# Modulation units of a two-block transformer kernel: 27 of them on VectorE, none in the norms' pauses, turned later and in other PSUM banks

## The reference

```python
c_act = jax.nn.silu(c)
for i in range(DEPTH):                                          # 2 layers
    mod = (c_act @ mod_w[i] + mod_b[i]).reshape(B, 3, 3, D)     # 9216 values a layer
    shift, scale, gate = mod[:, :, 0], mod[:, :, 1], mod[:, :, 2]
    h = modulate(rms_norm(x, norm_g[i, 0]), shift[:, 0], scale[:, 0])
    x = x + 0.5 * gate[:, 0, None, :] * swiglu(h, ffn_w_gate[i, 0], ffn_w_up[i, 0], ffn_w_down[i, 0])
    h = modulate(rms_norm(x, norm_g[i, 1]), shift[:, 1], scale[:, 1])
    y = fox_attention(h, ...) if i == 0 else dilated_attention(h, ...)
    x = x + gate[:, 1, None, :] * y
    h = modulate(rms_norm(x, norm_g[i, 2]), shift[:, 2], scale[:, 2])
    x = x + 0.5 * gate[:, 2, None, :] * swiglu(h, ffn_w_gate[i, 1], ffn_w_up[i, 1], ffn_w_down[i, 1])
```

## Time and profile before

| | |
|---|---|
| time, median of 3 runs | 2241.78 us (2241.42 to 2245.81) |
| profiled execution | 2246.45 us, of which the span of its instructions is 2244.8 us |
| busy: TensorE, its weight loads, VectorE, ScalarE, GpSimd | 96%, 84%, 66%, 48%, 7% |
| mean granted clock of TensorE | 0.987 of full speed |
| chain of work that ended last | TensorE 87%, ScalarE 5%, VectorE 5% |

### The profile page before, as it was taken

One profiled execution on the slowest core, in us unless ns is written; L12 is line 12 of the kernel. 1 busy time (PEld: TensorE's weight loads), 2 busy tenths in 40 slices (PEclk: granted clock), 3 DMA queues, 4 the chain that ended last, 5 costly groups with the idle time before them and its releaser, 6 DMA issues.

```text
span 2244.8 us, 33167 instructions
## 1 busy us (share of the span) xinstructions
PE 2149.6 (96%) x14132; PEld 1892.1 (84%) x14132; DVE 1484.3 (66%) x1939; ACT 1084.6 (48%) x1220; POOL 147.5 (7%) x180
## 2 busy tenths in 40 slices
PE   7999898999999999899999999999999999999998
PEld 5998665998799778687799887897998878988996
DVE  4677666776677666666665455567786655677874
ACT  4443465443444344645544335644555357435552
POOL 0311110111011100000000011000000110000000
PEclk9999999999999999999999999999999999999999
DMA  9977662977687756245275565534655564436551
GB/s 346 300 274 252 251 230 76 299 262 262 202 279 271 245 206 215 86 156 182 87 230 179 197 224 169 169 123 165 208 182 196 177 222 132 169 136 220 178 180 55
DMA packets 264259, 448.62 MB, mean 200 GB/s; under 512 B 11520, under 2 KB 147008, under 8 KB 263856
## 3 DMA queue, kind: packets, MB, share of 16 engines
q1 hardware_dynamic: 246784, 382.93, 51.5%
q0 software_dynamic: 17040, 62.46, 7.7%
q10 hardware_dynamic: 288, 1.11, 0.1%
HBM read 445.40 MB, written 1.06 MB: 199 GB/s over the span
## 4 chain that ended last, share of the span: by engine, by line
PE 87%; ACT 5%; DVE 5%; issue 1%; DMA 1%; POOL 0%; SPq 0%; ACTq 0%; DVEq 0%; POOLq 0%
PE ps L1494 85%; DVE wlo L1924 2%; ACT whi L1719 2%; PE ps L1685 1%; PE ps L1652 1%; ACT S L1719 1%; ACT L1719 1%; ACT xs L1719 1%; ACT xhi L1719 0%; DMA raw<-in_fox_w_in 0%; DMA raw<-in_mod_w 0%; PE ps L1642 0%; DVE S L2072 0%; DVE x L1974 0%; PE ps L1602 0%
## 5 line engine op out<-in xcount | busy, mean ns | idle before, releaser
L1924 DVE TENSOR_TENSOR wlo<-raw,whi 128x2048 fp32r<-128x2048 f32 (+1 forms) x339 | 769.6, 2278 | 402.8 <-ACT whi L1719 402.6
L1719 ACT ACTIVATE whi<-raw 128x2048 fp32r<-128x2048 f32 (+1 forms) x339 | 640.9, 1895 | 389.8 <-PE ps L1494 361.3
L1494 PE MATMUL ps<-xhi,whi 128*128 128x256 f32 x2632 | 650.5, 287 | 8.1 <-DVE wlo L1924 3.5
L1494 PE MATMUL ps<-xhi,wlo 128*128 128x256 f32 x2632 | 644.7, 285 | 0.0
L1494 PEld LDWEIGHTS ps<-xhi,whi 128*128 128x128 f32 x2632 | 508.8, 193 | 14.2 <-issue 4.8
L1494 PEld LDWEIGHTS ps<-xhi,wlo 128*128 128x128 f32 x2632 | 509.1, 193 | 1.8 <-issue 1.4
L1494 PE MATMUL ps<-xlo,whi 128*128 128x256 f32 x2632 | 344.3, 283 | 0.1
L1494 PEld LDWEIGHTS ps<-xlo,whi 128*128 128x128 f32 x2632 | 327.6, 192 | 0.5 <-DVE xlo L2038 0.3
L1494 PE MATMUL ps<-whi,xhi 128*128 128x512 f32 x736 | 297.1, 404 | 18.2 <-ACT xhi L1719 11.2
L1494 PE MATMUL ps<-wlo,xhi 128*128 128x512 f32 x736 | 291.3, 396 | 0.0
L1494 PE MATMUL ps<-whi,hhi 128*128 128x512 f32 x528 | 211.3, 400 | 5.7 <-DVE hlo L2048 4.1
(11 more groups left out here) (233 smaller groups left out, 1942.0 us busy)
## 6 DMA issues: line engine op xcount, KB each, us to landing
raw<-in_w_in SPq DMA_DIRECT2D x52, 1024.0 KB, 5.1
raw<-in_ffn_w_gate SPq DMA_DIRECT2D x88, 512.0 KB, 4.7
raw<-in_ffn_w_up SPq DMA_DIRECT2D x88, 512.0 KB, 5.9
raw<-in_ffn_w_down SPq DMA_DIRECT2D x44, 1024.0 KB, 5.0
raw<-in_w_up SPq DMA_DIRECT2D x88, 512.0 KB, 4.9
raw<-in_dil_w_in SPq DMA_DIRECT2D x36, 1024.0 KB, 5.2
raw<-in_mod_w SPq DMA_DIRECT2D x28, 1024.0 KB, 7.0
nbuf<-in_mod_w POOLq DMA_DIRECT2D x44, 512.0 KB, 5.2
```

What stands on the lines that cost most here:

```text
L1494: return nc.tensor.matmul(o, lhs, rhs, start=start, stop=stop, skip_group_check=True)
L1719: return nc.scalar.activation(o, i, func, **kw)
L1924: V.tensor_tensor(wlo[:, s["c"], 0:s["n"]], raw[:, s["slot"], 0:s["n"]], whi[:, s["c"], 0:s["n"]].bitcast(F32), ALU.subtract).then_inc(sem ...
```

## The change

- The first FFN gets 9 units on VectorE, the second and the third 8, the fourth 2: 27. Five fewer are computed on TensorE.
- No unit is computed in a norm's pause (`in_norm` goes, with its two pieces in the weight stream).
- The forgetting attention's projections have three units, one after each, instead of four; the dilated attention's have two instead of one.
- In FFN (0,0) `run_work` takes two and three parts in turn in the up projection (`work_rate`), elsewhere two as before.
- There is a third sum `macc`, in the last quarter of `xs`.
- The first down piece (`down(0)`) no longer lowers the counts of finished units (`age=False`), so a unit that ended with the up projection is turned behind that piece, in G3 or G2, and not ahead of it.
- After a norm whose turned x lay in G0, G1, D0, D1 the second projection's banks are (G0, G1), before (G2, G3).

```diff
@@ __init__
-        self.acc_free = [None, None]
+        self.acc_free = [None] * 3
+        self.work_turn, self.work_rate = 0, (2, 2)
@@ run_turns, run_work
-    def run_turns(self, mod_only=False):
+    def run_turns(self, mod_only=False, age=True):
...
-        for entry in self.acc_turns:
+        for entry in self.acc_turns if age else ():
             entry[0] -= 1
...
-    def run_work(self, n=2):
+    def run_work(self, n=None):
+        n, self.work_turn = n or self.work_rate[self.work_turn], 1 - self.work_turn
@@ mod_part
-        acc = self.n_units % 2
+        acc = self.n_units % 3
@@ begin_units
-        self.pair = 0
-        self.first_pair = (D2, D3) if self.turn_banks[0] == G0 else None
+        self.pair = int(self.turn_banks[0] == G0)
+        self.first_pair = (D2, D3) if self.pair else None
@@ down
         if q == 0:
-            self.run_turns()
+            self.run_turns(age=False)
@@ Tail
-        plan.run_work(len(plan.work))
+        plan.run_work(len(plan.work) + 1)
@@ stage_order
-        in_norm = {("ffn", 0, 1): (0, 16), ("ffn", 1, 0): (1, 6), ("ffn", 1, 1): (1, 16), ("mix", 0): (0, 11), ("mix", 1): (1, 14)}
-        on_vector = {(0, 0): [(0, u) for u in range(4, 11)], (0, 1): [(0, 17)] + [(1, u) for u in range(6)],
-                     (1, 0): [(1, u) for u in range(7, 14)], (1, 1): [(1, 17)]}
-        fill = {0: [(0, u) for u in range(12, 16)], 1: [(1, 15)]}
+        on_vector = {(0, 0): [(0, u) for u in range(4, 13)], (0, 1): [(0, 16), (0, 17)] + [(1, u) for u in range(6)],
+                     (1, 0): [(1, u) for u in range(6, 14)], (1, 1): [(1, 16), (1, 17)]}
+        fill = {0: [(0, 13), (0, 14), (0, 15)], 1: [(1, 14), (1, 15)]}
@@ mix
-                        for m in fl[:2 if r == 1 else 1] if hh == 0 else ():
+                        for m in fl[:1] if hh == 0 else ():
@@ lay_out, stage "norm"
-                md = s["m"]
-                self.mod_unit(*md, (D3 if self.turn_banks[0] == D0 else G3) - md[1] % 2, 1)
@@ lay_out, stage "gateup"
-                self.work_on = True
+                self.work_on, self.work_rate = True, (2, 3) if (i, s["j"]) == (0, 0) else (2, 2)
@@ build
-        macc = [mod_rows[:, 1, :], xs[:, 1, 0:512]]
+        macc = [mod_rows[:, 1, :], xs[:, 1, 0:512], xs[:, 1, 512:D]]
```

More of the change, by code:

```diff
@@ L1067, in ffn @@
             else:
-                step("norm", i=i, s=2 * j, m=in_norm["ffn", i, j])
+                step("norm", i=i, s=2 * j)
             step("mods", units=on_vector[i, j])
@@ L1077, in mix @@
             fl = list(fill[i])
-            step("norm", i=i, s=1, m=in_norm["mix", i])
+            step("norm", i=i, s=1)
             if i == 0:
@@ L1146, in stage_pieces @@
                     self.piece("w", list(half(q, k0)))
-        elif k == "norm" and s["m"]:
-            self.piece_unit(a["mod_w"][s["m"][0]], 512 * s["m"][1], kind="m")
         elif k == "mod":
```

## The result

| | before | after |
|---|---|---|
| time, median | 2241.6 us (2240.05 to 2245.81, 4 runs) | 2263.57 us (2262.7 to 2267.12, 4 runs) |
| ratio to before, 95% interval | | 1.009 (1.0076 to 1.0104) |
| profiled execution / its span | 2246.45 / 2244.8 us | 2263.08 / 2261.8 us |
| mean granted clock | 0.987 | 0.978 |

The account below looks back on a forecast made before the run. The prediction took TensorE, busy 96% of the span, as the bound. Gains 19.1 − pauses 3.2 − tail 10.9 = 5.0 us less than the profiled 2246.45; against the median 2241.78 it forecast 2236.8 us, range 2229 to 2244.

Parts of the forecast that it names:

- What costs nothing: Five more units on VectorE, 31 us, lie beside TensorE: VectorE needs 5.0 us per up piece, TensorE 5.8.
- a wait for wlo inside the first up projection: Sign named for a wrong forecast: the profile showing a wait for the low weights there; no size given.
- The rival of VectorE as the bound: FFN (0,0): 7.8 us at a 6.3 landing against TensorE's 9.3; decides from about 7.8; counted within slower, 0.15.
- FFN (0,0)'s first down piece: VectorE empties the bank ahead of the gating; 0.5 of the 1.82 wait stays: gain 1.3, and 1.5 of clock.
- The tail: End of FFN (0,0): five leftover parts make TensorE stand 9.0 us, with 1.9 of low clock: 10.9 together.
- The holes that go: TensorE's waits at first down pieces, second projections and the forgetting's projections shrink or go: gains of 19.1 us.
- The late turn: Holes ahead of the first down pieces of FFN (0,0), (0,1) and (1,0) go: 8.9 us.
- The gate's turn behind the norms: Before second projections a gate's turn falls from 1.80 to 0.45 us: gain 1.35, at two places.
- The fill: Forgetting attention's projections: one unit instead of two side by side, unit (0,12) turned in the FFN: gain 4.6 us.
- All else: Everything outside the up and down projections of FFN (0,0): forecast difference −13.1 us.
- The pauses: Norm pauses without a unit: TensorE idle 3.6 us, where it was 1.77; two get dearer by 1.6: 3.2.
- The fourth case: Slower, by the clock alone: each of five pauses costs 2.75 us, giving 2248 us; chance 0.15.

Follow-up runs that it names:

- e1: Changed kernel without the second and later loads of modulation weights in FFN (0,0), VectorE's work kept whole: 2236.22 us, 0.9968 of before.
- e2: Changed kernel with eight units in FFN (0,0) and unit (0,12) back among the forgetting attention's projections: 2253.68 us, 1.0046 of before.
- e4: Kernel before with the later turn alone (`age=False` and the third sum): 2232.75 us, 0.9947 of before.
- e5: Kernel before with the own banks alone, second projections after the norms writing to (G0, G1): 2240.64 us, 0.9986 of before.
- e15: Kernel before with both the later turn and the own banks, all units where they were: 2230.21 us, 0.9946 of before.
- e8: Changed kernel with four places of one part, and four parts behind each down piece of FFN (0,0): 2238.55 us, 0.9978 of before.
- e9: Changed kernel with eight units in FFN (0,0), unit (0,12) among the forgetting's projections, and four places of one part: 2243.36 us, 0.9999 of before.
- e6: Changed kernel with the two load buffers cut into four places of one part, same work and bytes: 2246.16 us, 1.0018 of before.
- e12: Changed kernel with FFN (0,0) as before, plus 7 to 16 matmuls of constants filling each of five norm pauses: 2230.63 us, 0.9937 of before.
- e10: Changed kernel with FFN (0,0) as before, plus 24 matmuls of constants in each of five norm pauses: 2240.75 us, 0.9981 of before.
- e13: Changed kernel with eight units and 2 and 4 parts in FFN (0,0), four places, (0,11) in its pause, constants in five pauses: 2225.15 us, 0.9913 of before.
- e14: e13 without the matmuls of constants in the pauses: 2232.14 us, 0.9953 of the kernel before.

## Why the prediction was wrong

- **The step that failed** stands under "What costs nothing": "VectorE needs 2.28 for the low part of the weights ..., 0.8 for the gating and its split ... and 1.9 for 2.5 parts: 5.0", against 5.8 of TensorE. That is a sum of busy times, 10 us a pair. In order on its engine a pair takes 11.55 (e1), 9.7 of it busy, since two round trips to ScalarE, 0.70 and 1.11, stand in it, which no busy time shows. The 1.6 us a pair that I took for spare were gone before the first landing was late, and "three weight buffers give it some slack" had nothing to refill it. The trace of before has both waits in every pair between 100 and 150 us. The sign that I had named for wrong, "a wait for wlo inside the first up projection", is what the trace then showed, three times.
- **The rival of VectorE as the bound** had the right engine and place, and a wrong point of decision, "only from a landing of about 7.8 on": it weighed loads against TensorE's time as if waiting and working overlapped. They don't, on an engine that works in order. Landings of 4.1 to 7.6 us, median 5.9, in this stretch (5.4 and 6.4 over the whole kernel) were enough. I gave it no chance of its own.
- **FFN (0,0)'s first down piece**: "I keep 0.5 of the 1.82" became 6.95: VectorE does empty the bank ahead of the gating, as I had it, but it comes there late. Without loads (e1) that wait is 0.41 and the stretch gains 2.6, forecast 2.8.
- **The tail** was right in mechanism and size: 10.23 us of standing against 9.0, 12.9 in all against 10.9, gone when FFN (0,0) has eight units and not nine (e2).
- **The holes that go**: right at 552 and 755. The late turn gave 11.9 for 8.9 forecast (e4). The gate's turn behind the norms fell to 0.45, but the stretch of FFN (1,1) where 1.35 was forecast gained 0.7 in e5 and e15 and lost 0.9 in the changed kernel, and the second block lost 1.5.
- **The fill**: 4.6 forecast; the rows "rest" with three fills and with four differ by 4.9 (changed kernel, e2) to 7.7 (e8, e9, where the larger holds the clock of the next point).
- **All else** came to −9.8 for −13.1, out of errors that partly cancel: the late turn gave more, the banks less. And between the norm behind FFN (0,0) and the next one the changed kernel is 4.3 us longer than e6, which has the same units there: its clock is 0.84 and 0.66 in the two stretches of 10 us from 390, and 1.00 in e6 at that place. My sum has no term for it. e9 has such a stretch there too and e8 has none, and what draws the clock down stays open.
- **The pauses**: each has a hole of 3.2 to 3.9, where 3.6 was worked out, and a low stretch behind it, which costs 0.6 and 1.65 us in the two windows that had none. The fourth case, 2.75 a pause, is not seen. The Trainium skill, "TensorE: Matmul & The Clock Gate", section "Part 4: PE-mode transpose", has it that transposes don't count as PE-busy in the same way; e12 shows that two groups of eight with work between them leave the clock at 1.00, so here the idle time decides.
- **The range** was drawn from the tail, the holes and the clock. None of them reaches 2263; the term that did stood in the text at nothing.

## What to carry to other kernels

Work that is to hide on a second engine must be fitted into that engine's order, not its busy time: take from the timeline the way from one repetition to the next, with each short wait in it, and count a round trip to another engine as work. If what is left is less than one late transfer, an engine that works in order passes that lateness on to all behind it. Here more and smaller buffers gave back 11.1 of 13.8 us at the same work; half a part less per piece gave back all of it, and 7 us of it came back elsewhere. And when a stage has an end, ask what is left over there: units that don't divide by the stage's slots stand bare on the path.

## What was unexpected of the hardware

- A load of 256 KB over GpSimd's queue landed after 5.0 and 5.6 us, one of 512 KB after 5.4 and 6.4. The Trainium skill, "DMA: Bandwidth & Descriptors", section "Anatomy of one DMA — SWDGE (gpsimd) path", gives about 2.0 us and the bytes by 436 GB/s; an estimate from it is 2.6 and 3.2. The small difference agrees (0.6 by the estimate, 0.4 and 0.8 measured), the level doesn't: here SyncE's weights run beside it, and what part of it they are was not tried.
- Fifteen matmuls of 128 x 128 fp32 constants have 30 records and take 3.5 us, 0.23 each.
- Filled pauses held the clock at 1.00 behind all five (e10, e12, e13). A comparison of e13 with e14 puts the five low stretches at 0.4% together, some 1.8 us each, near the 1.5 that I read from the earlier trace rows.
